# Bias rows' copies and counters' first transfers in later stages, key statistics and transposes one column group later

## The reference, cut to what matters

```
# first block
h = rmsnorm(x);  p = h @ w_in               # q, latent kv, indexer q/k/w, gates, mixing gates
ckv = rmsnorm(latent);  k_a, v_a = split(ckv @ w_kv_up)
ik = layernorm(i_k);  k_a, k_b, k_c = rmsnorm per head
o_a = attention over the 128 keys the indexer picks (+ T5 bias row of the distance)
o_b = sliding window attention (+ T5 bias row);  o_c = attention over 256 memory tokens
x = x + (gated sum of o_a, o_b, o_c through w_up) @ w_o
# second block
8 heads dilated attention (+ T5 bias row), 8 heads neighbourhood attention (+ rpb)
x = layernorm(ALPHA * x + out @ w_out_2)
```

## Time and profile before

| | |
|---|---|
| median of three runs | 2747.0 us |
| the profiled execution | 2748.4 us |
| its span, first to last instruction | 2746.9 us |
| mean granted TensorE clock | 0.984 |
| PE busy | 2651.1 us, 97% |
| DVE busy | 1191.5 us, 43% |
| ACT busy | 765.5 us, 28% |
| POOL busy | 249.7 us, 9% |
| DMA | 348.8 MB, mean 127 GB/s |

### The profile page before, as it was taken

One profiled execution on the slowest core, in us unless ns is written; L12 is line 12 of the kernel. 1 busy time (PEld: TensorE's weight loads), 2 busy tenths in 40 slices (PEclk: granted clock), 3 DMA queues, 4 the chain that ended last, 5 costly groups with the idle time before them and its releaser, 6 DMA issues.

```text
span 2746.9 us, 34039 instructions
## 1 busy us (share of the span) xinstructions
PE 2651.1 (97%) x12748; PEld 2132.9 (78%) x12748; DVE 1191.5 (43%) x2113; ACT 765.5 (28%) x1092; POOL 249.7 (9%) x385
## 2 busy tenths in 40 slices
PE   6959999998999999999999999999999999999998
PEld 5758888887777778888788888777777777777787
DVE  4636222222335775545455332444444444434425
ACT  5321221222332332323222222332233223222321
POOL 4111000000000110111000000000001111211000
PEclk8989999999999999999999999999999999999999
DMA  7454433333343443435444444232232222323432
GB/s 219 114 163 153 143 107 115 115 122 110 111 141 114 148 139 123 161 138 194 151 162 159 158 148 135 90 98 94 94 107 87 92 89 93 99 99 105 180 117 93
DMA packets 70545, 348.80 MB, mean 127 GB/s; under 512 B 11699, under 2 KB 11699, under 8 KB 42275
## 3 DMA queue, kind: packets, MB, share of 16 engines
q1 hardware_dynamic: 38148, 241.28, 25.9%
q0 software_dynamic: 32320, 106.46, 12.2%
HBM read 298.74 MB, written 50.45 MB: 127 GB/s over the span
## 4 chain that ended last, share of the span: by engine, by line
PE 92%; DMA 2%; DVE 2%; ACT 1%; issue 1%; POOL 0%; POOLq 0%; SPq 0%; ACTq 0%; DVEq 0%
PE bank L391 25%; PE bank L393 25%; PE bank L392 25%; PE bank L1069 5%; PE bank L955 2%; PE bank L937 2%; PE bank L1093 2%; PE bank L925 1%; DMA w_raw<-wst 1%; DVE w_lo L380 1%; PE bank L824 1%; PE bank L805 1%; PE bank L786 1%; DMA mem_raw<-mem_t 1%; PE bank L764 1%
## 5 line engine op out<-in xcount | busy, mean ns | idle before, releaser
L380 DVE TENSOR_TENSOR w_lo<-w_raw,w_hi 128x2048 fp32r<-128x2048 f32 x211 | 486.9, 2308 | 527.8 <-ACT w_hi L375 527.8
L391 PE MATMUL bank<-act_a,w_hi 128*128 128x512 f32 (+1 forms) x1672 | 660.8, 395 | 5.5 <-ACT stage L1285 4.1
L393 PE MATMUL bank<-act_a,w_hi 128*128 128x512 f32 (+1 forms) x1672 | 652.5, 390 | 0.0
L392 PE MATMUL bank<-act_a,w_lo 128*128 128x512 f32 (+1 forms) x1672 | 651.8, 390 | 0.0
L391 PE MATMUL bank<-act_b,w_hi 128*128 128x512 f32 x1280 | 505.2, 395 | 7.7 <-DVE act_b L1956 5.2
L375 ACT ACTIVATE w_hi<-w_raw 128x2048 fp32r<-128x2048 f32 x210 | 401.0, 1910 | 395.9 <-PE bank L393 316.0
L393 PE MATMUL bank<-act_b,w_hi 128*128 128x512 f32 x1280 | 499.6, 390 | 0.0
L392 PE MATMUL bank<-act_b,w_lo 128*128 128x512 f32 x1280 | 499.2, 390 | 0.0
L391 PEld LDWEIGHTS bank<-act_a,w_hi 128*128 128x128 f32 (+1 forms) x1672 | 314.2, 188 | 79.9 <-issue 16.1
L393 PEld LDWEIGHTS bank<-act_a,w_hi 128*128 128x128 f32 (+1 forms) x1672 | 313.9, 188 | 66.8
L392 PEld LDWEIGHTS bank<-act_a,w_lo 128*128 128x128 f32 (+1 forms) x1672 | 314.5, 188 | 63.3
(11 more groups left out here) (286 smaller groups left out, 2205.7 us busy)
## 6 DMA issues: line engine op xcount, KB each, us to landing
w_raw<-wst SPq DMA_DIRECT2D x215, 1024.0 KB, 4.9
mix_d<-stage POOLq DMA_DIRECT2D x24, 512.0 KB, 3.0
mixg<-mix_d POOLq DMA_DIRECT2D x8, 1536.0 KB, 6.8
b<-rows_2d POOLq DMA_DIRECT2D x16, 448.0 KB, 7.4
x_raw<-x_t SPq DMA_DIRECT2D x8, 512.0 KB, 8.2
q_d<-stage POOLq DMA_DIRECT2D x8, 512.0 KB, 3.2
g_d<-stage POOLq DMA_DIRECT2D x8, 512.0 KB, 3.2
qb<-q_d POOLq DMA_DIRECT2D x16, 256.0 KB, 3.9
```

What stands on the lines that cost most here:

```text
L380: dve.tensor_tensor(w_lo[s][:], w_raw[s][:], w_hi[s][:].bitcast(F32), ALU.subtract).then_inc(lo_ready, 1)
L391: pe.matmul(out_ap, l_hi, r_hi, start=start, stop=False)
L392: pe.matmul(out_ap, l_lo, r_hi, start=False, stop=False)
L393: return pe.matmul(out_ap, l_hi, r_lo, start=False, stop=stop)
```

## The change

- `first_d`: the eight first transfers are issued behind the stores of the memory values.
- The four copies of the bias rows are issued one by one behind the four stores of groups 8 to 11. `rows_2` lies elsewhere, the waits of ScalarE and VectorE for `brow_out` are gone, and POOL waits for it before the first bias load.
- ScalarE splits chunk 14 and copies the latent before it waits for chunk 15; it no longer waits for the stored keys before group 12.
- VectorE empties the value units and splits chunk 17 before the indexer key's layer norm; roots follow the same order on ScalarE.
- Statistics of the A keys and the memory keys, and all transposes of keys, stand one column group later; the halves of a weight chunk come ahead of the copies to `stage`. `hi2`/`lo2` are written out as their two splits.

The diff, with unchanged lines and the bodies of `iq_out` and `keys_out` (moved up, the same) left out:

```diff
@@ -178,7 +178,7 @@
...
-        rows_2 = sb_at("rows_2", [HEADS_2, ROW_2], Y + 4 * KB)
+        rows_2 = sb_at("rows_2", [HEADS_2, ROW_2], Y + 16 * KB)
@@ -727,12 +727,12 @@
...
-            proj(G_IQ, 0, turn_short_keys)
-            proj(G_IQ + 1, 1, lambda: turn_keys((0, 1)))
-            proj(G_IQ + 2, 0, lambda: turn_keys((2, 3)))
-            proj(G_IQ + 3, 1, turn_mem_keys)
+            proj(G_IQ, 0)
+            proj(G_IQ + 1, 1, turn_short_keys)
+            proj(G_IQ + 2, 0, lambda: turn_keys((0, 1)))
+            proj(G_IQ + 3, 1, lambda: turn_keys((2, 3)))
+            proj(G_Q, 0, turn_mem_keys)
...
-            proj(G_Q, 0)
@@ -1207,11 +1207,11 @@
...
+            split_hi(act, 14, 0)
+            act.wait_ge(cf_s, 1)
+            copy(ckv_t[0][:], ckv_f[:]).then_inc(sp_h, 1)
...
-            act.wait_ge(cf_s, 1)
-            copy(ckv_t[0][:], ckv_f[:]).then_inc(sp_h, 1)
-            split_hi(act, 14, 0)
@@ -1228,28 +1228,28 @@
...
-            root(2, 4)
...
-            root(3, 8)
-            act.wait_ge(brow_out, 64)
...
+            root(2, 4)
+            root(3, 8)
...
+            split_hi(act, 2 * G_IQ + 3, 1)
...
-            split_hi(act, 2 * G_IQ + 3, 1)
...
+            root(5, 8)
+            split_hi(act, 2 * G_IQ + 5, 1)
...
-            split_hi(act, 2 * G_IQ + 5, 1)
...
-            root(5, 8)
+            split_hi(act, 2 * G_IQ + 7, 1)
...
-            hi2(G_IQ + 3)
+            split_hi(act, 2 * G_IQ + 8, 0)
@@ -1267,7 +1267,6 @@
...
-            act.wait_ge(kst_k, 256)
@@ -1652,8 +1651,30 @@
...
+            def key_sums(blocks):
+                for b in blocks:
+                    sum_sq(k_nat[:, b, :].rearrange("p (h d) -> p h d", d=P), HEADS_A, P, HEADS_A * b)
...
+            kv_out(1)
+            split_lo(dve, 2 * G_IQ + 1, 1)
@@ -1670,8 +1691,6 @@
...
-            kv_out(1)
-            split_lo(dve, 2 * G_IQ + 1, 1)
@@ -1685,68 +1704,49 @@
...
-            for b in range(2):
-                sum_sq(k_nat[:, b, :].rearrange("p (h d) -> p h d", d=P), HEADS_A, P, HEADS_A * b)
-            dve.wait_ge(sp_t, 3)
-            dve.tensor_scalar(ik_t[:], bank[6][:], pcol("ik_g"), pcol("ik_b"), ALU.mult, ALU.add).then_inc(sp_o, 2)
...
-            dve.wait_ge(sp_t, 4)
-            for kv in range(2):
-                last = scaled(kt_b[:, kv, :], bank[4 + kv][:], pcol("k_b"))
-            last.then_inc(sp_o, 1)
-            for b in range(2, TB):
-                sum_sq(k_nat[:, b, :].rearrange("p (h d) -> p h d", d=P), HEADS_A, P, HEADS_A * b)
+            key_sums(range(TB))
...
+            split_lo(dve, 2 * G_IQ + 3, 1)
+            iq_out(G_IQ, 0)
...
-            dve.wait_ge(brow_out, 64)
...
-            iq_out(G_IQ, 0)
-            split_lo(dve, 2 * G_IQ + 3, 1)
-            keys_out((0, 1))
+            dve.wait_ge(sp_t, 3)
+            dve.tensor_scalar(ik_t[:], bank[6][:], pcol("ik_g"), pcol("ik_b"), ALU.mult, ALU.add).then_inc(sp_o, 2)
...
-            iq_out(G_IQ + 1, 1)
-            split_lo(dve, 2 * G_IQ + 5, 1)
+            dve.wait_ge(sp_t, 4)
+            for kv in range(2):
+                last = scaled(kt_b[:, kv, :], bank[4 + kv][:], pcol("k_b"))
+            last.then_inc(sp_o, 1)
...
-            keys_out((2, 3))
-            split_lo(dve, 2 * G_IQ + 6, 0)
+            split_lo(dve, 2 * G_IQ + 5, 1)
+            iq_out(G_IQ + 1, 1)
...
+            split_lo(dve, 2 * G_IQ + 6, 0)
+            keys_out((0, 1))
+            split_lo(dve, 2 * G_IQ + 7, 1)
...
-            split_lo(dve, 2 * G_IQ + 7, 1)
+            split_lo(dve, 2 * G_IQ + 8, 0)
+            keys_out((2, 3))
...
-            dve.wait_ge(sp_t, 9)
-            for n in range(2):
-                last = scaled(kt_c[:, 2 * n:2 * n + 2, :], bank[4 + n][:].rearrange("p (h t) -> p h t", t=MEM), pcol("k_c"))
-            last.then_inc(sp_o, 1)
-            split_lo(dve, 2 * G_IQ + 8, 0)
...
+            def mem_keys_out():
+                dve.wait_ge(sp_t, 9)
+                for n in range(2):
+                    last = scaled(kt_c[:, 2 * n:2 * n + 2, :], bank[4 + n][:].rearrange("p (h t) -> p h t", t=MEM), pcol("k_c"))
+                last.then_inc(sp_o, 1)
@@ -1770,7 +1770,10 @@
...
-                lo2(G_Q + s)
+                split_lo(dve, 2 * (G_Q + s) + 1, 1)
+                if s == 0:
+                    mem_keys_out()
+                split_lo(dve, 2 * (G_Q + s) + 2, 0)
@@ -2178,9 +2181,6 @@
...
-            for n, done in enumerate(staged_out + o_out + x1_out + y_out):
-                pool.dma_start(first_d[n:n + 1, :], con_in[n:n + 1, 0:16]).then_inc(done, 16)
@@ -2195,9 +2195,10 @@
...
-            pool.wait_ge(pe_s, 6)
-            for dst, src in ((rows_a, rows_1a[:]), (rows_b, rows_1b[:]), (rows_2d, rows_2[:]),
-                             (rows_n, rpb_in.rearrange("h r c -> h (r c)"))):
+            for n, done in enumerate(staged_out + o_out + x1_out + y_out):
+                pool.dma_start(first_d[n:n + 1, :], con_in[n:n + 1, 0:16]).then_inc(done, 16)
...
+            def bias_rows(dst, src):
@@ -2210,10 +2211,6 @@
...
-            pool.wait_ge(sp_o, 3)
-            for j in range(ITEMS_B):
-                pool.dma_start(k_d[j], kt_b[:, j // 3, :]).then_inc(kst_k, 16)
@@ -2223,12 +2220,21 @@
...
-            for g in range(G_IQ, G_IQ + 3):
-                iq_store(g)
+            pool.wait_ge(pe_s, 6)
+            iq_store(G_IQ)
+            bias_rows(rows_a, rows_1a[:])
+            pool.wait_ge(sp_o, 3)
+            for j in range(ITEMS_B):
+                pool.dma_start(k_d[j], kt_b[:, j // 3, :]).then_inc(kst_k, 16)
+            iq_store(G_IQ + 1)
+            bias_rows(rows_b, rows_1b[:])
+            iq_store(G_IQ + 2)
+            bias_rows(rows_2d, rows_2[:])
...
+            bias_rows(rows_n, rpb_in.rearrange("h r c -> h (r c)"))
@@ -2292,6 +2298,7 @@
...
+            pool.wait_ge(brow_out, 64)
...
```

More of the change, by code:

```diff
@@ L1653, in kv_out, with iq_out, keys_out @@
                     dve.tensor_copy((v_nat if kind else k_nat)[:, b, 0:384], bank[KV_BANK[u % 2]][:, 0:384]).then_inc(kv_dve, 1)
+            def iq_out(g, s):
+                summed(g)
+                dve.wait_ge(staged_out[s], 16 * ((g - G_IQ) // 2) + 16)
+                dve.tensor_copy(stage[s][:, 1, :], bank[2 * s + 1][:]).then_inc(ev_dve, 1)
+            def key_sums(blocks):
+                for b in blocks:
+                    sum_sq(k_nat[:, b, :].rearrange("p (h d) -> p h d", d=P), HEADS_A, P, HEADS_A * b)
+            def keys_out(blocks):
+                for b in blocks:
+                    dve.wait_ge(sp_t, 5 + b)
+                    bk = 4 + 2 * (b % 2)
+                    cols = slice(b * P, (b + 1) * P)
+                    scaled(kt_a[:, 0:4, cols], bank[bk][:].rearrange("p (h t) -> p h t", t=P), pcol("k_a"))
+                    scaled(kt_a[:, 4:6, cols], bank[bk + 1][:, 0:256].rearrange("p (h t) -> p h t", t=P), pcol("k_a"))\
+                        .then_inc(sp_o, 1)
             kv_out(0)
             split_lo(dve, 2 * G_IQ, 0)
+            kv_out(1)
+            split_lo(dve, 2 * G_IQ + 1, 1)
             dve.wait_ge(sp_t, 2)
```

## The result

The changed kernel takes 2708.2 us at the median of four runs (2703.93 to 2709.62), the kernel before 2747.7 (2746.95 to 2749.18): a ratio of 0.9851, 95% interval 0.9839 to 0.9864. That is 39.5 us faster. The steps at the latent and in the projection groups came out within 0.2 us. What was missed lies at the start, in the part priced at nothing.

A forecast was written before the change was run, and what follows sets the result against it. PE, 97% busy, was taken as the bound, so only its gaps and slow clock could be won. 21.2 + 3.5 + 4.5 + 0.2 = 29.4 us off the 2747.0 median gave 2717.6, range 2713 to 2724.5.

The forecast's parts named there:

- The steps at the latent and in the projection groups: Latent to first projection group: that group starts 29.2 us earlier; inside the groups, 0.2 us saved.
- the part priced at nothing: Start of the kernel: moving the eight first transfers away was taken as 0 us, possibly some 3 us of gain.
- (a): Long gap at the latent: bias rows moved and ACT reordered, so PE starts at 151.05 instead of 172.22; 21.2 us saved.
- (b): Clock: the units after the two long gaps would each take 2.08 us; 3.5 us saved.
- The chain of pure computation: At the latent: ready at 146.3, then ACT's copy, DVE's half and w_lo, with PE starting at 151.05.
- rival 4: Key and value units: clock stays low after three short gaps, 14.3 us less gain, 2732 us; chance 0.01.
- (c): Third value unit: its copies go before the index key's chain on DVE; 4.5 us saved, 0.75 of the gap stays.
- (d): Ahead of w_hi of chunk 25: ACT's wait for stored keys goes; 0.2 us saved.
- (f): Projection groups: bias-row copies in new places stay within the weights' 25.9 us cover; cost 0, range 0 to 6.0 us.
- (e): Chunk 19: statistics and transposes one group later; w_lo ends near 198.2, PE wants it at 202.5; cost 0.
- (g): Start: eight 64-byte first transfers leave it; taken as 0 us, between 0 and some 3 us of gain.
- rival 3: Start was held by the first transfers: 1 to 4 us more gain, 2714 to 2717 us; chance 0.05.

The follow-up runs named there:

- e3: Kernel before with only the four bias-row copies moved behind the stores of groups 8 to 11: 2735.9 us, ratio 0.996.
- e4: Kernel before with only ACT's order changed, chunk 14 split and latent copied before the wait for chunk 15: 2742.65 us, ratio 0.9985.
- e8: Changed kernel with DVE's index-key chain ahead of the value units' copies again, and ACT's root ahead of its own: 2713.5 us.
- e9: Kernel before with the bias-row copies moved and ACT's wait for the stored keys removed: 2723.6 us.
- e10: Changed kernel with all four bias-row copies issued together behind the store of group 9: 2706.0 us, ratio 0.9845.
- e1: Changed kernel with the eight 64-byte first transfers back at the very start: 2717.95 us, ratio 0.9899.
- e2: Kernel before with only the first transfers moved behind the stores of the memory values: 2735.3 us, ratio 0.996.
- e7: Changed kernel with the eight first transfers at the start, to HBM, each of 16 rows of 512 bytes: 2707.5 us.
- e12: Changed kernel with the eight first transfers at the start, 4-byte writes to HBM, each element 4 KB from the next: 2706.75 us, ratio 0.9847.
- e6: Changed kernel with the eight first transfers at the start, written to SBUF instead of HBM: 2707.6 us.
- e5: Changed kernel with two of the eight first transfers at the start: 2707.5 us.
- e11: Changed kernel with the eight first transfers at the start, 4-byte writes to HBM, each transfer 64 KB from the next: 2710.5 us, ratio 0.9867.

## Why the prediction was wrong

- **(a) and (b), right.** For (a) 21.2 us were forecast; the gap went from 21.83 to 0.64, which is 21.2. For (b) 3.5 were forecast; the two units took 1.5 and 1.8 less, 3.3. The chain of pure computation (latent, ACT's copy, DVE's half, w_lo) ended as counted. The copies as the cause are shown by e3 (PE at 151.29, expected 151.75) and e4. The clock of 1.00 behind the short gaps speaks against rival 4.
- **(c), right.** 4.5 forecast, 5.29 - 0.76 = 4.5 found; e8 shows it apart.
- **(d), right in this change, and mis-sized as an edit.** It was priced at 0.2 by the trace of before. With the copies moved in the kernel before, that wait is worth 10 to 14 us (e3 against e9). The working of (f) said that nobody needs the stores queued behind the copies for 20 us; that holds only because this edit took away the one who did.
- **(e), right.** w_lo of chunk 19 ended at 187.49, forecast 198.2 less the 10.4 of the start, 187.8; PE's first matmul with it came at 193.48. The last sum of the keys and that w_lo:

```profile
181.94 0.95 DVE L1623 TENSOR_REDUCE ssk<-sq_w 128x6 f32<-128x768 f32 x1
...
185.20 2.29 DVE L380 TENSOR_TENSOR w_lo<-w_raw,w_hi 128x2048 fp32r<-128x2048 f32 x1 [2.10 <-ACT w_hi L375]
```

- **(f), right in its sum, one detail off.** No PE gap. The chunk that met rows_2d was not 25, which was issued 2 us ahead of it and was through, but 26; it landed in 14.6 us, just under the 15 to 24 forecast. The copy itself took 20.9 us from its issue, where 18.4 were reckoned on the engines. The prediction read the earlier trace rows as 14 us of weights shut out; a weight chunk was asked for only from 131.96 on, so it was 10. In the changed kernel it was nearly 7, in e10 over 8. The Trainium skill, page "DMA: Bandwidth & Descriptors", section "SWDGE vs HWDGE vs iDMA", has each engine go round its queues at packet boundaries, and lets a packet hold up to 64 descriptors. The prediction took what the profile calls a packet for that packet, and got 8 us for a whole chunk. No run here shows how the two relate, so these 7 to 10 us neither bear the rule out nor contradict it.
- **(g), the step that failed.** The eight transfers were priced by their own share of the engines, 0.15 us, with 0 to 3 as the range, and rival 3 got 1 to 4 us and 5%. They cost 10.4 (39.5 less the 29.1 of e1; 11.8 in the kernel before, e2), because they hold up the others' packets, not because they take time. The trace of before had it in rows that the prediction didn't use: `mem_raw` landed in 11.0 us at the median and 19.8 at the most where it takes 5.7 without them, and from 8 to 12 us SP's queue moved 61 packets with 57% of the engines' time. The rest of the sum stands: e1, the change without (g), gains 29.1 where 29.4 were forecast. The Trainium skill, page "DMA: Bandwidth & Descriptors", section "Specifications", says that below 512 bytes a transfer does a read-modify-write. That fits e7, where packets of 512 bytes cost nothing; but e12, with 4-byte writes 4 KB apart and no cost either, shows that the size alone isn't it. No run here shows a read-modify-write as such.

## What to carry to other kernels

A tiny transfer isn't priced by its bytes, nor by its own time on the engines: look at how long the packets beside it take, and compare a transfer's landing in that stretch with the same transfer elsewhere. If its data doesn't matter, as here, SBUF or places far apart cost nothing (e6, e12). A bulk copy such as those out of 6 or 16 partitions here can shut out the weight stream for 7 to 10 us; put it where the next weight has more time than the copy takes, and look for every wait whose stores then queue behind it. A wait that costs PE 0.2 us today may be the price of tomorrow's move (10 to 14 us in e3).

## What the runs showed of the hardware

- 128 writes of 4 bytes into the same 512 bytes of HBM within the first 20 us cost 10 to 12 us of kernel time (e1, e2); from 8 to 12 us the loads beside them moved 0.18 MB (e1) instead of 1.60. 32 of them (e5), 128 to SBUF (e6), 128 of 512 bytes (e7) or 128 at 4 KB from each other (e12) cost no kernel time that can be told. In e5, and with sixteen to each 64 bytes (e11, 0 to 4 us), the loads were held up all the same: 0.93 and 0.53 MB.
- With copies from 6 or 16 partitions to HBM in flight, SP's queue moved no packet, with a weight chunk issued, for 10 us in the kernel before, nearly 7 in the changed one and over 8 in e10, at 92 to 97% of the engines. POOL's queue moved 82 GB/s meanwhile (before, 128 to 142) and 106 (changed, 239 to 249).
